# The first 20 microseconds of a three-layer transformer forward pass: order of the two token halves, and products of zeros on TensorE

## What is computed

```
x = x + 0.5 * rmsnorm(swiglu(rmsnorm(x, g[0]), ffn_w_in[0, 0], ffn_w_out[0, 0]), g[1])

rmsnorm(x, g)          = x * rsqrt(mean(x * x, -1) + 1e-6) * g
swiglu(h, w_in, w_out) = (silu((h @ w_in)[:, :2816]) * (h @ w_in)[:, 2816:]) @ w_out
```

## Time and profile before

| | |
|---|---|
| median of three runs | 1783.08 us |
| the profiled execution, whole | 1782.63 us |
| its span, first to last instruction | 1780.8 us |
| TensorE busy | 1708.7 us, 96% |
| VectorE busy | 1089.9 us, 61% |
| ScalarE busy | 884.6 us, 50% |
| first product with a weight | 16.48 us after the span's start |

### The profile page before, as it was taken

How to read it: one execution, slowest core, us unless ns; L and a number is a source line. 1 busy time by engine, 2 the same in 40 slices (tenths; PEclk the granted TensorE clock), 3 DMA queues, 4 the chain that set the end, 5 groups by cost and what they waited for, 6 DMA issues and landing times.

```text
span 1780.8 us, 28106 instructions
## 1 busy us (share of the span) xinstructions
PE 1708.7 (96%) x11942; PEld 1565.6 (88%) x11942; DVE 1089.9 (61%) x1419; ACT 884.6 (50%) x1373; POOL 178.9 (10%) x192
## 2 busy tenths in 40 slices
PE   7999999999998999999989999999999999999996
PEld 6899799799996998989879997799989888799995
DVE  5455667678777544668665556655557685755555
ACT  4344556544555455453554445544445445544444
POOL 0000001309002002920010001100000000000001
PEclk9999999999999999999999999999999999999999
DMA  6655444455554544540445554465555322454552
GB/s 231 226 200 194 155 153 143 162 189 188 190 189 160 175 172 145 183 148 25 177 160 189 179 183 169 172 214 201 176 188 178 133 105 97 160 211 176 183 194 86
DMA packets 51084, 300.97 MB, mean 169 GB/s; under 512 B 6072, under 2 KB 12688, under 8 KB 17168
## 3 DMA queue, kind: packets, MB, share of 16 engines
q1 hardware_dynamic: 50800, 298.66, 47.2%
q0 software_dynamic: 160, 0.52, 0.1%
HBM read 298.08 MB, written 1.09 MB: 168 GB/s over the span
## 4 chain that ended last, share of the span: by engine, by line
PE 71%; DVE 9%; ACT 9%; DMA 6%; issue 2%; POOL 1%; SPq 1%; DVEq 0%; POOLq 0%; ACTq 0%
PE PS L1853 68%; DMA raw<-in_w 5%; DVE wlo L1141 4%; ACT whi L655 3%; PE PS L1856 2%; ACT wk L698 1%; ACT SC L789 1%; DVE xn L1230 1%; POOL st L547 1%; DMA SC<-in_pT 1%; DVE X L1222 1%; ACT SC L877 1%; DVE SC L1385 0%; POOL st L540 0%; PE PS L1982 0%
## 5 line engine op out<-in xcount | busy, mean ns | idle before, releaser
L1141 DVE TENSOR_TENSOR wlo<-raw,whi 128x1024 fp32r<-128x1024 f32 x528 | 661.6, 1260 | 438.1 <-ACT whi L655 436.4
L655 ACT ACTIVATE whi<-raw 128x1024 fp32r<-128x1024 f32 x528 | 551.8, 1055 | 410.7 <-PE PS L1853 237.9
L1853 PE MATMUL PS<-xhi,whi 128*128 128x256 f32 x2520 | 717.2, 285 | 5.1 <-DVE wlo L1141 4.3
L1853 PE MATMUL PS<-xhi,wlo 128*128 128x256 f32 x2520 | 712.1, 283 | 0.0
L1853 PE MATMUL PS<-xlo,whi 128*128 128x256 f32 x2520 | 705.2, 283 | 0.0
L1853 PEld LDWEIGHTS PS<-xhi,whi 128*128 128x128 f32 x2520 | 484.1, 192 | 12.8 <-DVE wlo L1141 6.6
L1853 PEld LDWEIGHTS PS<-xhi,wlo 128*128 128x128 f32 x2520 | 484.2, 192 | 0.0
L1853 PEld LDWEIGHTS PS<-xlo,whi 128*128 128x128 f32 x2520 | 480.4, 192 | 2.1
L1853 PE MATMUL PS<-whi,hhi 128*128 128x512 f32 x544 | 170.6, 395 | 2.5 <-DVE wlo L1141 2.5
L1853 PE MATMUL PS<-wlo,hhi 128*128 128x512 f32 x544 | 168.6, 391 | 0.0
L1853 PE MATMUL PS<-whi,hlo 128*128 128x512 f32 x544 | 168.3, 391 | 0.0
(11 more groups left out here) (264 smaller groups left out, 1445.5 us busy)
## 6 DMA issues: line engine op xcount, KB each, us to landing
raw<-in_w SPq DMA_DIRECT2D x264, 1024.0 KB, 4.8
gr<-in_rows SPq DMA_DIRECT2D x23, 512.0 KB, 3.8
SC<-scratch SPq DMA_DIRECT2D x1, 2048.0 KB, 12.1
SC<-scratch SPq DMA_DIRECT2D x2, 1024.0 KB, 11.4
X<-in_x SPq DMA_DIRECT2D x2, 512.0 KB, 4.9
xn<-in_sc SPq DMA_DIRECT2D x2, 512.0 KB, 6.8
out<-xn SPq DMA_DIRECT2D x2, 512.0 KB, 2.7
SC<-in_pT SPq DMA_DIRECT2D x3, 256.0 KB, 4.0
```

Of the source, the lines that this page charges most:

```text
L655: a.activation(whi[:, u % NSPLIT, :], raw[:, u // 2 % NRAW, u % 2 * HU:u % 2 * HU + HU], ACT.Copy).then_inc(s_hi, 1)
L1141: v.tensor_tensor(wlo[:, u % NSPLIT, :], src, hi.bitcast(f32), SUB).then_inc(s_lo, 1)
L1853: return pe.matmul(o, l, r, start=start, stop=stop)
```

## The change

The load of X[1] is issued directly behind that of X[0]. ScalarE and VectorE call `use(-AHEAD)`, which by `upto(v)` covers exactly half unit 0, behind turn 10 and turn 12 of stage 0: ScalarE copies half unit 0 between its evictions of half 0 and of half 1, VectorE subtracts it between its evictions of the same halves. VectorE first sets `nil`, 128 columns of `rot`, to zero. TensorE multiplies `nil` by itself into PSUM bank 0: 12 times at the beginning, 3 times each behind the first and the second sum of squares of half 0 and behind the factor of half 0, and 4 times behind the stage. Nothing reads these results.

```diff
+        s_nil = sem("s_nil")
...
+        nil = rot[:, 0, 0:2, :].rearrange("p i n -> p (i n)")
...
             sp.dma_start(X[:, 0, :], x[0, 0:128, :]).then_inc(l_x[0], 16)
+            sp.dma_start(X[:, 1, :], x[0, 128:256, :]).then_inc(l_x[1], 16)
             row(0)
             sp.dma_start(idt[:, :], idn).then_inc(l_id, 16)
-            sp.dma_start(X[:, 1, :], x[0, 128:256, :]).then_inc(l_x[1], 16)
             weights(-AHEAD - 1)
...
-            settle(0)
+            settle(0, {10: lambda: use(-AHEAD)})
             ffn(0)
...
-            take_turns(0, steps)
+            v.memset(nil, 0.0).then_inc(s_nil, 1)
+            take_turns(0, steps, {12: lambda: use(-AHEAD)})
...
+            def nil_products(n):
+
+                for _ in range(n):
+                    mm(PS[:, 0, 0:128], nil, nil, True, True)
+
+            q.wait_ge(s_nil, 1)
+            nil_products(12)
+            q.wait_ge(s_sq, n_sq(0, 0, 0))
+            nil_products(3)
+            q.wait_ge(s_sq, n_sq(0, 0, 1))
+            nil_products(3)
+            q.wait_ge(s_r2, n_one(0, 0))
+            nil_products(3)
             settle(0)
+            nil_products(4)
             bg.add(bias_tiles(0))
             ffn(0)
```

## The result

The changed kernel takes 1777.98 us (median of 20 runs), the kernel before 1781.62 us beside it (20 runs): ratio 0.9978, 95% interval 0.9972 to 0.9985, so 3.9 us less, between 2.7 and 5.0. The profiled execution after took 1780.86 us, of which 1779.1 span. So the time by itself doesn't choose between the two; the traces do.

The account below looks back on a forecast made before the run. TensorE, busy 1708.7 of 1780.8 us, bounds the kernel behind a serial start without products until 16.48. Earlier start 2.9 plus clock 2.1 gives 5.0: 1783.08 - 5.0 = 1778.1 us, range 1776.0 to 1781.7.

Parts of the forecast that it names:

- the earlier start: First weight product in TensorE's row: at 13.57 us instead of 16.48, 2.9 us of the forecast 5.0 us gain.
- the clock's part: Products of half unit 0 at the high instead of the low clock: 2.1 us of the forecast 5.0 us gain.
- Order of the loads: Start loads: X[1] lands at 5.8 (latest 6.76), row 0 about 8.1, unit 0 unchanged at 10.7; costs half 0's norm 1.0 us.
- Half 1: Second half in stage 0: factor ready about 8.4 (9.8 if X[1] lands at 6.76), norm 9.55 to 10.95, 1.2 us earlier.
- Split between the halves: Half unit 0 between the evictions of both halves: first product at 13.57, half unit 0 done at 16.45 instead of 21.5.
- Zeros: Products of zeros in TensorE's waits before the first weight product: no cost on the chain, and they bring the high clock.
- Clock: TensorE from the start: clock rises at about 5 to 6 us and is still high at 13.57; chance 0.60.
- the pause ahead of 543.36: Precedent later in TensorE's row: 1.70 us idle, then 1.32 of transposes, with granted clock 1.00 behind it.
- Whether the gain lasts: Weight loads behind the start: half unit 5's margin falls from some 6 us to 1.2, no pause; stall around 79.29 moves whole.
- The low clock at the first product: Rival: half unit 0 takes 5.0 us as before, 13.57 to 18.6; gain 2.9, 1780.2 us; chance 0.25 with the last rival.
- zeros in the way: Rival: products of zeros cost 0.55 each and delay the transposes, half unit 0 done at 23.6; 1785.2 us; chance 0.05.
- A late row 0: Rival: row 0 lands at, say, 9.5, shifting VectorE's line 1.4 us; about 1781.5 us; chance 0.10 with gain partly given back.

Follow-up runs that it names:

- the version: The change, plus weight unit 10 issued between the two big loads of the first bias stage and unit 11 behind the second: 1773.84 us, ratio 0.9951 to the kernel before.
- order and split: The change without any product of zeros: ratio 0.9977 to the kernel before (0.9966 to 0.9987), first product 13.23, half unit 0 done at 18.0.
- zeros alone: The kernel before with only the products of zeros added, loads and weight split as before: ratio 0.9989 (0.9978 to 1.0000), half unit 0 done at 18.2.
- split and zeros: The change without the new load order, row 0 and identity ahead of X[1] again: ratio 0.9975 to the kernel before, half unit 0 done at 17.4.
- twelve-zeros kernel: The change with only the first twelve products of zeros, the later 3+3+3+4 left out: ratio 0.9969 to the kernel before, half unit 0 done at 17.2.
- with 48: The change with 48 products of zeros at the beginning instead of 12: ratio 1.0001 to the kernel before, first product 19.21, half unit 0 done at 22.1.

## Why the prediction was right

**The time.** 1778.1 forecast, 1777.98 measured. The closeness is in part luck: the forecast subtracted 5.0 from a median of three runs, 1783.08, which 20 runs put at 1781.62; the measured difference is 3.9 (2.7 to 5.0). So the forecast size, 5.0, is at the upper end of what was measured. Of its two parts only the earlier start, 2.9, is needed to come into that interval; that the clock's part is there, too, rests on the traces.

**Order of the loads.** X[1] at 5.8 was 5.7, unit 0 at 10.7 was 10.3. Row 0 came at 7.5, not 8.1, and so cost half 0 only 0.4 us (7.51 for 7.09), not 1.0. The norm did wait for it, as the bracket of its row says.

**Half 1.** Its norm at 9.55 was 9.38, but with another last cause: not VectorE and the row, but GpSimd, whose two steps took 0.83 and 0.84 there, where I had reckoned with about 1.0 us for both. A slip beside it did no harm: if X[1] had landed at 6.76, the factor would by the same rows have been ready at about 9.3, not 9.8; the sum doesn't use it.

**Split between the halves.** First product at 13.57 was 13.18, and VectorE's evictions and subtraction are the last steps, as forecast. The end at 16.45 was 16.0, so 5.5 us instead of 5.0.

**Zeros.** Their cost on the chain is nothing, as taken: they end at 8.2, and the transposes start at 8.40 when `xn` is there. The room is small: the same zeros took 0.7 us longer in the version's trace, where the clock rose later, and ended only as the transposes began, at 8.67. A call costs 0.43 at first and 0.22 later, inside the bounds 0.12 and 0.55. What they bring was named as the spacing alone, 2.1 us; beside order and split it is 1.9. Alone they also shorten the transposes; the prediction had both of their times, but didn't count the difference as a gain.

**Clock.** High at the first product, in all three traces with all 25 products of zeros and the new load order (the change twice, the version), and in the two with the old one (zeros alone, split and zeros). The argument for it was weak, though, and that part is luck. I likened the stretch to the pause ahead of 543.36, behind which the clock was 1.00. In the second trace of the change the same transposes stand at 536.64, behind 1.71 us idle for 1.70, and there the granted clock is 0.50 at 538 to 540 us. So this precedent changes from one execution to the next. And I let transposes count for something, which no run here settles. The twelve-zeros kernel shows what the prediction didn't say: it is the products of zeros behind the squares, the factor and the stage, taken together, that carry the clock across.

**Whether the gain lasts.** Nothing is waited for until the pause at 71 to 74 us, and that one moved along whole (2.75 after, 2.48 before). At 338 us 5.4 to 5.8 us are left against one trace of the kernel before and 3.8 to 4.3 against the other. What the runs show, 3.9 and 4.3 (ratios 0.9978 and 0.9975), is lower than the 5.5 won at the start; both intervals reach 5.0. By the granted clocks of all runs some 0.7 us of this, with a standard error of 0.5, may be more falls of the clock. Whether anything else is lost, these runs don't settle.

**Rivals.** The low clock at the first product was made to happen with twelve zeros; zeros in the way, with 48. A late row 0 did not come: it landed at 7.4 to 7.6 in the traces with the new order.

## What to carry to other kernels

Read the start of a kernel as a single file of steps and ask of each edit which step is last once the others have moved: the same edit (zeros) was worth about 2.8 us alone and 1.9 beside the two others, in the traces. Ask as well whether the runs can see it: order and split without zeros ran as fast as the whole change. Where one execution's later pauses cost 1.7 us or nothing by chance, compare traces up to the first such pause, and the whole only over many runs. Loads that are wanted later (here 3 MB in two issues) should not stand in a queue ahead of the next weight load: two issues moved ahead were worth as much as the whole new start.

## What the runs showed that was not expected

GpSimd's operation on 128x1 elements takes 0.30 us while VectorE is idle, and 0.82 while VectorE runs a norm beside it. Its first operation for half 1 in the kernel before, and in the kernel after:
```profile
9.84 0.30 POOL L540 TENSOR_SCALAR st<-st 128x1 f32<-128x1 f32 x1 [2.86 <-ACT wk L698]
...
7.61 0.82 POOL L542 TENSOR_SCALAR st<-st 128x1 f32<-128x1 f32 x1 [0.55 <-ACT wk L700]
```
The operation behind it takes 0.56 before, at 10.23, and 0.83 after, at 8.51. The new load order brought the two engines together, which cost half 1's factor 0.8 us in both traces of the change and in that of order and split. It is a matter of a tenth of a microsecond: in the four other traces with the new order the norm began 0.02 to 0.07 us after GpSimd's first operation had, which then took 0.30, and VectorE went on into half 1 without a pause. With the split and its early copy that gave a first product at 12.8 to 12.9 instead of 13.1 to 13.2.

The column of the granted clock says 1.00 from the start of every trace, also where the spacing of starts is 0.21 us. It can be believed from the first change that it shows; in the twelve-zeros kernel it does show 0.50 from 10 to 16 us.
